# Three reorderings at stage borders of a two-block transformer kernel: output weights of the first attention, a tile's norm before the first feed-forward, the last merge of the second token mixer

## What is computed

```python
mod = jax.nn.silu(c) @ ada_w[layer] + ada_b[layer]          # shifts, scales and gates
yx, yc = windowed_gqa(hx, hc, attn_w_in, attn_w_out, ...)   # 16 heads, 4 key heads, softmax with a sink
x = x + g1 * yx                                             # gated addition
hx2 = rms_norm(x, norm2_g[layer]) * (1.0 + sc2) + sh2       # norm ahead of the feed-forward
x = x + g2 * conv_glu(hx2, ffn_w_up, ffn_conv_w, ffn_conv_b, ffn_w_down)
```

```python
merged = (sigmoid(g_a) * (out_a @ w_proj_a) + sigmoid(g_b) * (out_b @ w_proj_b))
mix = merged @ w_out
x = layer_norm(alpha * x + mix, ln1_g, ln1_b)
x = layer_norm(alpha * x + moe_ffn(x, ...), ln2_g, ln2_b)
```

## Time and profile before

| | |
|---|---|
| median of 3 runs | 2429.98 us (2429.1 to 2431.84) |
| profiled execution | 2437.23 us, span 2435.0 us |
| mean granted TensorE clock | 0.982 |
| busy | PE 2299.1 us, DVE 949.6, ACT 747.7, POOL 69.3 |
| DMA | 603.14 MB, mean 248 GB/s |
| instructions | 32307 |

### The profile page before, as it was taken

How to read it: one execution, slowest core, us unless ns; L and a number is a source line. 1 busy time by engine, 2 the same in 40 slices (tenths; PEclk the granted TensorE clock), 3 DMA queues, 4 the chain that set the end, 5 groups by cost and what they waited for, 6 DMA issues and landing times.

```text
span 2435.0 us, 32307 instructions
## 1 busy us (share of the span) xinstructions
PE 2299.1 (94%) x13342; PEld 1514.5 (62%) x13342; DVE 949.6 (39%) x1584; ACT 747.7 (31%) x1113; POOL 69.3 (3%) x60
## 2 busy tenths in 40 slices
PE   5999899999999999999999899999999999999997
PEld 3944687787788899899798786333333333333332
DVE  4478543444143458666454655111111111111112
ACT  4366442333124433355345652111111111111101
POOL 0000000000000135000000000000000000000000
PEclk8999999999999999999999999999999999999999
DMA  9278135332222331245563168999999999999996
GB/s 347 70 277 242 35 122 197 115 104 104 87 104 70 104 105 36 90 153 176 187 220 127 54 181 345 398 428 428 429 428 429 428 429 428 429 428 429 428 429 289
DMA packets 142483, 603.14 MB, mean 248 GB/s; under 512 B 6720, under 2 KB 52032, under 8 KB 117664
## 3 DMA queue, kind: packets, MB, share of 16 engines
q1 hardware_dynamic: 142368, 601.52, 63.2%
HBM read 600.44 MB, written 1.05 MB: 247 GB/s over the span
## 4 chain that ended last, share of the span: by engine, by line
PE 76%; DMA 12%; DVE 5%; ACT 5%; issue 1%; POOL 0%; SPq 0%; DVEq 0%; ACTq 0%; POOLq 0%
PE bank L1054 74%; DMA arena<-in_w_up 5%; DMA ring<-in_w_up 5%; DMA ring<-in_ada_w 1%; PE bank L1281 1%; ACT arena L2387 1%; ACT w_high L2227 0%; DVE hw_low L2780 0%; ACT arena L2296 0%; ACT wide_p L2284 0%; PE bank L1702 0%; POOL arena L931 0%; DVE arena L2716 0%; DMA ring<-in_ffn_w_up 0%; ACT hw_high L2064 0%
## 5 line engine op out<-in xcount | busy, mean ns | idle before, releaser
L1054 PE MATMUL bank<-arena 128*64 128x512 f32 (+7 forms) x2256 | 442.1, 511 | 38.2 <-ACTq L792 21.6
L1054 PE MATMUL bank<-hT_high,w_split 128*128 128x512 f32 (+1 forms) x1408 | 345.7, 337 | 3.6 <-DVE hT_low L2458 3.6
L1054 PEld LDWEIGHTS bank<-arena 128*64 128x64 f32 (+2 forms) x2256 | 173.6, 156 | 275.2 <-issue 200.4
L1054 PE MATMUL bank<-ring,arena 128*64 128x512 f32 (+1 forms) x1248 | 301.5, 598 | 19.3 <-ACT arena L2387 11.8
L1054 PEld LDWEIGHTS bank<-hT_high,w_split 128*128 128x128 f32 x1408 | 242.1, 190 | 35.1 <-issue 4.1
L1054 PE MATMUL bank<-hT_low,w_split 128*128 128x512 f32 (+1 forms) x704 | 236.6, 336 | 0.0
L3156 DVE TENSOR_SCALAR arena<-bank 128x512 f32<-128x512 f32 x32 | 22.1, 692 | 542.6 <-PE bank L1054 542.4
L1054 PEld LDWEIGHTS bank<-ring,arena 128*64 128x64 f32 (+1 forms) x1248 | 99.9, 142 | 205.7 <-issue 182.3
L1054 PE MATMUL bank<-freed_w,arena 128*64 128x512 f32 x768 | 170.3, 595 | 6.0 <-ACT arena L2387 5.5
L1054 PEld LDWEIGHTS bank<-hT_low,w_split 128*128 128x128 f32 x704 | 133.6, 190 | 13.8 <-issue 0.2
L1054 PEld LDWEIGHTS bank<-freed_w,arena 128*64 128x64 f32 x768 | 53.4, 137 | 115.9 <-issue 104.2
(11 more groups left out here) (420 smaller groups left out, 3946.3 us busy)
## 6 DMA issues: line engine op xcount, KB each, us to landing
ring<-in_ada_w SPq DMA_DIRECT2D x24, 2048.0 KB, 8.3
ring<-in_w_gate SPq DMA_DIRECT2D x24, 2048.0 KB, 24.5
arena<-in_w_up SPq DMA_DIRECT2D x24, 2048.0 KB, 27.5
ring<-in_w_down SPq DMA_DIRECT2D x24, 2048.0 KB, 28.9
arena<-in_w_down SPq DMA_DIRECT2D x24, 2048.0 KB, 28.1
ring<-in_w_up SPq DMA_DIRECT2D x24, 2048.0 KB, 26.0
arena<-in_w_gate SPq DMA_DIRECT2D x24, 2048.0 KB, 25.1
ring<-in_ffn_w_up SPq DMA_DIRECT2D x42, 1024.0 KB, 7.8
```

What stands on the lines that cost most here:

```text
L1054: return pe.matmul(o, l, r, start=start, stop=stop)
```

## The change

Four places change, none adds or removes an instruction. On ACT and DVE, piece 1 of the output weights of the first attention is split behind step 16 and not behind step 15. On DVE, `inverse_norm(0)` moves ahead of the last gated addition. On DVE, `merge(3)` moves ahead of `wo2_rest(2)`, and on ACT `merged_high(3)` ahead of `wo2_part(3)`.

```diff
@@ ACT, first attention
-                if i in (14, 15):
-                    out_high(i - 14)
+                if i in (14, 16):
+                    out_high((i - 14) // 2)
             out_high(2)
             out_high(3)
@@ ACT, merge
             merged_high(2)
             wo2_part(2)
+            merged_high(3)
             wo2_part(3)
-            merged_high(3)
@@ DVE, enter_first
                 weights_low(0, 0)
                 add_tile("wo0", 1, 0, GATE[(0, 0)])
+                inverse_norm(0)
                 add_tile("wo0", 1, 1, GATE[(0, 0)])
                 signal(gates_read)
-                inverse_norm(0)
                 inverse_norm(1)
@@ DVE, first attention
-                if i in (14, 15):
-                    out_low(i - 14)
+                if i in (14, 16):
+                    out_low((i - 14) // 2)
@@ DVE, merge
             merge(2)
             merged_low(2)
+            merge(3)
             wo2_rest(2)
-            merge(3)
             merged_low(3)
             wo2_rest(3)
```

## The result

The changed kernel is slower: 2435.99 us in the median of 16 executions (2433.58 to 2444.56), against 2431.46 of 16 executions of the kernel before (2428.01 to 2438.33). The ratio is 1.0022, 95% interval 1.0014 to 1.0030. The means differ by 5.0 us. I had forecast 2430.6 us and no change to be measured.

What follows compares the result with a forecast made beforehand. PE was taken to fill three quarters of the span, DMA an eighth, so only edits shifting PE or the experts' loads count. +0.56 + 0.4 - 0.33 = +0.6 us gave 2430.6 us for the median, range 2427.0 to 2433.2.

Steps and rivals of the forecast that it cites:

- A: End of first attention, weight piece 1 split behind step 16: projection 0.56 us later, range -1.38 to +0.56 us.
- From that product to the projection it is 3.81 us: Unit 15, value product of chunk 1 to projection: 278.92 - 275.11 us, added to the product's new start at 275.67.
- rival 2: Unit 15: PE's two waits of some 1.3 us lower its clock, projection starts at half speed, 1.4 to 2.8 us more; chance 0.15.
- Its 2.37 us: Taken as the shortest PE wait with a low clock behind it, so the clock counted as low behind 3.24 and 2.44 us.
- B: Border to the first feed-forward, norm of tile 0 ahead of the last addition: PE waits 0.3 to 0.5 us more, taken as +0.4.
- a gain has no room: Norm of tile 0: DVE's wait for ACT's root ends when it did, so tile 0's products still start at 333.76.
- C: Merge, last merge ahead of a subtraction: PE goes on 0.33 us earlier, waits 2.44 not 2.77, clock low; range -1.6 to 0.
- Rival 1: Clock stays full behind the shorter waits of unit 14, the merge or both; with both -2.6 us, 2427.4; chance 0.18.
- Rival 3: Loads of the experts or of earlier layers set their own pace, time stays at 2430.0 us; chance 0.12.
- the 0.03 and 0.04 for other causes: Chances left for a cause not listed reaching 4.9 us: 0.03 for faster, 0.04 for slower.

Runs made afterwards that it cites:

- A alone: Kernel before with only weight piece 1 of the output weights split behind step 16 on ACT and DVE: +0.9 ± 1.3 us, a second time +2.1 ± 1.3.
- A with B or C: Kernel before with piece 1's move plus the norm move (+5.2 ± 1.1 us), the merge move (+4.6 ± 1.2) or both (+5.5 ± 1.0 in the second series).
- the whole: The changed kernel with all its edits, against the kernel before, run in two series: means 5.0 us apart in the first, +5.5 ± 1.0 us in the second.
- B alone: Kernel before with only inverse_norm(0) moved ahead of the last gated addition: -1.2 ± 1.2 us.
- the second series of the whole change: The changed kernel with all its edits run once more beside the kernel before on the same chip: +5.5 ± 1.0 us, ratio 1.0021.
- the filled kernel: Kernel before with piece 1 split behind step 16 and PE's waits in units 14 and 15 filled with unread products: -0.5 ± 0.8 us.
- the further one: Kernel before with merge(3) and merged_low(3) both ahead of wo2_rest(2), and merged_high(3) ahead of wo2_part(3): -3.4 ± 1.1 us, ratio 0.9984.
- B and C: Kernel before with the norm move and the merge move, without the move of piece 1: -1.3 ± 1.0 us.
- the version with both gains: Kernel before with piece 1's split moved, its subtraction behind step 17, unread products in units 14 and 15, last low part before wo2_rest(2): -6.7 ± 0.8 us, ratio 0.9970.

## Why the prediction was wrong, step by step

**The step that failed: in A, the clock of unit 15.** "From that product to the projection it is 3.81 us" was taken from a unit that ran at 1.00 (the kernel before, 273.90 to 278.90), and moved to one in which PE waits twice. The expectation was +0.56 us for A; the runs say +1.7 ± 0.9 for A alone, 5.1 ± 0.5 for A with B or C, and +3.4 ± 0.5 over all. I had the mechanism as rival 2, "unit 15 costs PE its clock", and gave it 0.15 and 1.4 to 2.8 us for reaching into the projection. What it does is in the profiles: the clock falls within unit 15 in five of six executions with A, the unit itself loses 1.1 to 1.4 us by it (5.68 and 280.19 - 274.19 = 6.00 in the two profiles of the whole, and not 4.62, from copy to projection), and in three of the five the projection starts at half speed and loses another 2. I had argued that behind unit 15 as it was PE ran at full speed, "so short waits among turns did not cost the clock". But there PE waited 0.36 us ahead of its first value product, where it now waits 1.56. The row spoke of a wait a quarter as long.

The earlier trace rows misled me too. Its 2.37 us is not the shortest wait with a low clock behind it. Later in the same trace PE waits 1.62 us at 1392.51, and the clock is at 0.51 from 1394.20 to 1397.60; and there are two short waits among turns and products, of the size that I was weighing for unit 15. First the stretch of unit 15, then those two waits and the stretch behind them, all of the kernel before:

```profile
273.90:278.90 5.00, 3.64 (x24) 1.63 (x24) 1.53 (x3) 1.57 (x3) 0.00 (x0) 1.00 0.00 0
...
1415.24 0.65 PE L1054 MATMUL bank<-arena 128*64 128x256 f32 x4 [0.79 <-ACTq L792]
...
1417.20 0.35 PE L1054 MATMUL bank<-oA_high,pa_high 128*128 128x256 f32 x1 [1.30 <-DVEq L792]
...
1418.10:1421.50 3.40, 3.40 (x19) 3.40 (x18) 3.37 (x2) 3.34 (x4) 0.00 (x0) 0.51 1.06 233
```

So a row for rival 2 was there before the forecast. Nor is a wait's length enough to tell: in the profile of the changed kernel the clock stays at 1.00 behind a wait of 2.37 us at 99.11 and one of 2.92 us at 860.49, and in the profile of B alone it does behind these same waits of 0.80 and 1.30. What decides in which execution the clock falls was not found.

The Trainium skill, "TensorE: Matmul & The Clock Gate", section "A second HAM failure mode: psum-queue depth-cycling", describes a kernel whose clock goes up and down because PE idles briefly and often between groups. The trace of the second series of the whole change agrees: waits of 1.56 and 1.19 us with two groups of four instructions between them, and the clock at 0.50 for 10.2 us. The second profile of A alone, with waits of 1.59 and 1.20 us and a clock of 1.00, does not show it. The rule of the Trainium skill that I weighed (the same page, section "Why this matters for your kernels") is on longer idle stretches and says nothing of these. Going by it I would have left the clock full in unit 15, as I did, and the measurement decides against that.

**The other steps of A.** The waits came out as worked out: 3.24 us for unit 14, and 4.69 and not 4.71 us from rounding to copy. Unit 14 was rounded sooner than I had it, 266.45 - 261.24 = 5.21 us after PE's return and not 5.88, since the clock came back earlier (0.66 in the stretch from 261.20 to 266.20, against 0.50 in the earlier trace rows). With a full clock in both units the bound was -1.38 us, and the filled kernel shows -1.33 at the place.

**B** was to cost 0.4 us and costs nothing at the place. From the profile of the changed kernel, DVE at the border:

```profile
331.18 0.16 DVE L2441 RECIPROCAL stat<-stat 128x1 f32<-128x1 f32 x1 [1.66 <-ACT stat L1812]
...
331.70 0.69 DVE L2486 TENSOR_TENSOR arena<-bank,gb 128x512 f32<-128x512 f32 x1
...
334.78 0.16 DVE L2441 RECIPROCAL stat<-stat 128x1 f32<-128x1 f32 x1 [1.66 <-ACT stat L1812]
```

The addition stands behind the first reciprocal, as foreseen, and the second reciprocal follows 334.78 - 331.70 = 3.08 us later and not 3.22. What I had wrong is that "a gain has no room": PE begins tile 0 at 331.72, 6.14 us behind `weights_low`'s first piece (325.58), where it was 333.76 - 327.29 = 6.47. These 0.33 us cover the wait in the middle, and from that piece to the first product of the feed-forward it is 339.58 - 325.58 = 14.00 us, 0.19 less than before. The bias loads were late and cost nothing, by the cover that I had named: SP's next issue came at 345.83.

**C** was right at its own place and missed one behind it. The wait is 2.48 us for 2.44, the last low part comes 0.30 us earlier for 0.33 (16.73 us behind the first and not 17.03), and the clock is low behind it, as forecast. DVE of the changed kernel at the merge, against the earlier trace rows:

```profile
1443.37 2.29 DVE L3025 TENSOR_TENSOR hw_low<-ring,wo_high 128x2048 fp32r<-128x2048 f32 x1
1445.69 0.69 DVE L3039 TENSOR_TENSOR m_low<-arena,m_high 128x512 fp32r<-128x512 f32 x1
```

But then there is the routing, some 8 us behind the output product. The stretches there, first of the kernel before:

```profile
1483.00:1489.80 6.80, 6.80 (x27) 5.54 (x26) 2.82 (x16) 1.66 (x3) 0.33 (x1) 0.50 1.00 425
1489.80:1496.70 6.90, 5.96 (x43) 5.00 (x43) 5.91 (x19) 0.38 (x1) 0.00 (x0) 1.00 1.02 437
```

and of the changed kernel:

```profile
1477.20:1484.00 6.80, 6.80 (x26) 5.54 (x26) 2.83 (x16) 1.47 (x3) 0.14 (x1) 0.50 1.02 437
1484.00:1490.90 6.90, 6.22 (x22) 4.88 (x22) 5.87 (x19) 0.00 (x0) 0.00 (x0) 0.50 1.02 435
```

The clock falls some 7 us behind the last addition of the output product in both (1475.96 before, 1469.98 now), but stays low twice as long in the second. In six of the seven profiled executions with C as in the change, the stretch from the last addition of the output product (L3066) to the second expert's gate activation (L3156) is 3.0 us longer than in before, and in the seventh it is the same; without C's edit, or with the further one, it is between 1.6 us shorter and 1.3 us longer in nine. Over all 17 profiles the loss goes with the length of the low stretch there: 3.4 us low, 1.6 shorter than before (three profiles); 6.8, level (seven); 10.2, 1.3 longer (one); 13.7, 3.0 longer (six). In the mean C costs +1.0 ± 0.6 us, and in B and C, the kernel of the seventh profile, nothing; so the 3.0 is not there in every execution. PE's waits just ahead of the low stretch are 0.85 and 0.79 us before and 0.84 and 0.79 now, so they do not tell why it is longer, and how C's edit some 30 us earlier brings it about was not found. In the two profiles with the wait at the merge at 0.93 and 0.94 us the longer stretch did not occur.

**The rivals and the range.** Rival 1, a clock that stays full behind the shorter waits, was seen at neither place: it is low behind 3.24 and behind 2.48 us. Rival 3, a shift that is swallowed, is refuted: the version with both gains shows them whole. Rival 2 had the right mechanism with a price of 2432 to 2433.4 us, and the measured time is 2436: I left out that the unit itself slows down, and C's routing. Another 1.5 us is not the change's: the kernel before stands at 2431.46 in 16 executions and stood at 2429.98 in the three that I started from. The chances of my list already made 1.00, so the 0.03 and 0.04 for other causes had no room in it.

## What to carry to other kernels

One long wait of PE may cost less than a shorter one and two short ones in its place: count the waits of the stage, and price each stage from a row in which PE waits as it will wait then, not as it waits now. Look for that row in the whole trace, and for several short waits in a row as well as for one long one. Where the price hangs on the clock, one profile of each kernel tells the mechanism but not the mean; it takes many executions of both, and kernels that differ in that one wait alone. The remedy here was to take the work that only the next stage needs (the subtraction of piece 1) out of the last unit, and to take the last low part ahead of work that is not yet due.

## What the runs showed that I had not expected

- The same kernel, A alone, ran unit 15 at a granted clock of 1.00 in one execution (place -0.28 us) and at 0.50 in another (+3.35), with waits of 1.59 and 1.20 us in the first case and 1.56 and 1.19 in the second.
- Behind waits of 1.56 and 1.19 us the granted clock was at 0.50 for 10.2 us, longer than in the kernel before with its one wait of 5.18 us, where it was low from 264.4 to 271.2.
- Ten products that nobody reads, in a wait of 5.18 us that PE has anyway, gain 1.8 us at their place in the profile, where the clock stays at 1.00 behind them.
- Where the low clock falls moves whole executions. From the fourth gated addition to the first low part of the merge, five profiles with 27.3 us at 0.50 take 1132.5 to 1132.7 us, and four with 10.2 us take 1127.5 to 1128.5, whatever the edit.
- 150 executions of the kernel before spread from 2427.0 to 2440.5 us. With 12 of an edit and some 30 of the other, a difference of 3 us is barely told from none.
